# Block ends and two attention stages of a two-block transformer kernel: fewer column sums on TensorE, held-back first loads, queries loaded a stage early

## The chip, the cores and the metric

The kernel runs on one core of one Trainium2 chip as one program. The metric is the time of the whole program on the device in microseconds (us). The core has TensorE (matmuls, called PE in the profile, its weight loads PEld), VectorE (DVE), ScalarE (ACT), GpSimd (POOL) and SyncE (SP, which here only issues DMAs). Every engine runs its own list of instructions in order, and semaphores make them wait for each other.

## The reference, cut to what matters

Two blocks work on a sequence of 1024 tokens of width 1024 (`T` = 1024, `P` = 128). The first block runs twice (once with a recurrent mixer, once with a convolution mixer). Each of its two passes ends in the same few lines:

```python
h = layer_norm(DEEPNORM_ALPHA * h + mix @ w_out[i], ln_g[i], ln_b[i])
e = rms_norm(p[i] @ ple_w[i], ple_norm[i])
h = h + jax.nn.sigmoid(h @ ple_gate[i]) * e
```

`layer_norm` takes the mean and the mean square of the centred values over the 1024 channels; `rms_norm` takes the mean square of `p @ ple_w` over its 1024 channels.

The second block has two attentions side by side on the same input. `mla_attention` is causal attention with 8 heads of width 96. `nsa_attention` is the sparse one: 8 heads of width 64 in 2 groups, each query looks at compressed keys (made of windows of 32 tokens by a small two-layer network with weights `cmp_w1` and `cmp_w2`), at the 8 best blocks of 64 tokens, and at a window of 256 tokens; three gates mix the results:

```python
o = g[..., 0, :] * o_c + g[..., 1, :] * o_s + g[..., 2, :] * o_w
```

## The kernel before, in words

Everything is float32. Activations lie with channels on the 128 partitions and tokens along the free axis, so a sum over channels is a sum over partitions, which TensorE does with a matmul against a constant matrix `avg`. Large products use three matmuls of float32r parts (a high and a low part of weights and activations) for each tile; VectorE splits each weight tile (`divide`, lines 123 and 128). The program is a row of stages; between two stages stand a clearing of semaphores and a barrier of all engines.

**Block end** (`block_end`, line 5150; stage name `be`). It runs twice, near 1490 to 1755 us and near 2925 to 3195 us. TensorE does 24 products (`product`, matmuls on line 5250): 8 of `mix @ w_out` (g = 0 to 7, 48 matmuls each), 8 of `p @ ple_w` (g = 8 to 15, 12 matmuls each) and 8 of the gate (g = 16 to 23, 48 matmuls each). Around the middle the two norms are made:

- after product 8 a matmul with `avg` (line 5275) gives the mean, and VectorE subtracts it from the 8 tiles (line 5378);
- ScalarE squares each of the 8 centred tiles and each of the 8 tiles of `e` (`square`, line 5312), into one of two buffers `sq`. It also copies the 8 `e` tiles out of PSUM (`take_e`, line 5317);
- TensorE turns each of the 16 squared tiles into a column sum per 128 tokens: `add_squares` (line 5259) does 8 matmuls with the squares as weights and one column of `avg` as moving data. The layer norm's 8 go into `ln_cols`, the other 8 into `rm_cols`;
- when `ln_cols` is full, a small chain (VectorE line 5382, ScalarE square root line 5332, VectorE reciprocal line 5384) makes the factor, `spread` (line 5265, 8 matmuls) puts it on all partitions, VectorE multiplies the tiles (line 5395), ScalarE and VectorE make the high part (line 5322) and the low part (`lower_y`, line 5390) of each tile as moving data of the gate product.

The order on TensorE: product 8, mean, product 9, ten `add_squares` in a row (two of `e`, eight of the layer norm), product 10, `spread`, then products 11 to 15 with one `add_squares` after each, product 16 with the last one inside, second `spread`, products 17 to 23. A square may be written only after the buffer's last reader is done (`sq_used`).

**Dense attention** (`mla_select`, line 4135; stage name `mla`, 3806 to 4167 us). SP loads head 0's `q` and `k` (96 rows of 1024), the identity and the masks, head 0's `v`, then head 1, the weights of the compression (`w1` and others, 15 loads counted in `cmp_in`), heads 2 and 3, five tables and heads 4 to 7, without waiting. After that SP stores 16 output tiles as they come (`normed`). TensorE first makes the scores of units 0 and 1 (`row_scores`, lines 4368 and 4371); each waits for all three loads of its head, and its mask matmul for three small VectorE instructions (lines 4549 to 4551) that wait for identity and masks. Beside the attention, the compression (8 steps, line 4295) and the selection for the sparse attention run. POOL first issues two loads of queries for the selection, then sets the ones in `k` and `v`.

**Sparse attention** (`nsa_attention`, line 3799; stage name `nsa`, 4170 to 4580 us). SP loads `q` and `k` of both groups in 24 DMAs (lines 3887 and 3890, each row block twice, 6 MB in all). POOL loads identity, masks, `rows_in`, the selection, the gates, `v`, the compressed probabilities `pct` and `vc`. TensorE waits for the seven constants made by VectorE (`NMADE`) and for the first half of group 0's `q` and `k`, makes the first four chunks of scores (lines 3924 and 3929), and VectorE reduces each to maxima (lines 4020 and 4023) before the one PSUM buffer can be used again.

## Time and profile before

| | |
|---|---|
| median of 3 runs | 5513.8 us (5513.04 to 5519.81) |
| profiled execution | 5518.23 us, its span 5516.4 us |
| mean granted TensorE clock | 0.925 of full speed |
| PE busy | 88% of the span |
| DVE busy | 50% |
| ACT busy | 19% |

Times within the profile count from the span's start. The granted clock is 1.00 at 2.4 GHz and 0.50 at 1.2 GHz. A busy PE is not a PE at its peak: matmuls are pipelined, and one that waits for its weights counts as busy.

### The profile page before, as it was taken

To read this page: it belongs to the slowest core of one execution; us is meant where nothing else is said; L and a number is where in the kernel's file an instruction comes from. 1 tells how busy PE (TensorE), PEld (TensorE's weight loads), DVE (VectorE), ACT (ScalarE), POOL (GpSimd) and SP (SyncE) were. 2 spreads that over 40 slices of the span, in tenths; PEclk is the share of its full clock that TensorE was granted. 3 is DMA by queue.
4 is the path that set the end of the run, shared out by engine and by line. 5 is a ranking of instruction groups with operands and counts; after the bars stand their busy time and mean duration, and the time that the engine had idled before them with its cause. 6 is when DMAs were issued, how large, how long until landed. Compare 5 with 4: busy or idle time off the path is not lost. (4 is left out here: it accounts for less than half of the span.)

```text
span 5516.4 us, 89051 instructions
## 1 busy us (share of the span) xinstructions
PE 4851.6 (88%) x38472; PEld 3735.2 (68%) x38494; DVE 2746.4 (50%) x3664; ACT 1071.6 (19%) x1481; POOL 716.0 (13%) x646
## 2 busy tenths in 40 slices
PE   9996997999798997684867969998996998999999
PEld 7776887999586766343446847765653557788887
DVE  5776543444445886374664457232463335443332
ACT  2443221222321330000001221111221122110000
POOL 0002321111000460000000011011000000131330
PEclk9998998999789998796888889998997999999999
DMA  3443213111213333423223134136114004212213
GB/s 136 162 153 112 58 29 117 57 57 57 97 52 119 124 142 149 172 92 111 87 72 139 58 121 156 60 106 171 35 27 79 5 8 146 98 48 78 80 43 103
DMA packets 247271, 512.69 MB, mean 93 GB/s; under 512 B 35351, under 2 KB 118616, under 8 KB 246244
## 3 DMA queue, kind: packets, MB, share of 16 engines
q1 hardware_dynamic: 184580, 362.92, 20.3%
q0 software_dynamic: 31488, 110.53, 5.9%
q10 hardware_dynamic: 30816, 33.56, 1.7%
q8 instruction: 306, 5.01, 0.4%
q14 instruction: 81, 0.66, 0.0%
HBM read 353.70 MB, written 150.74 MB: 91 GB/s over the span
## 5 line engine op out<-in xcount | busy, mean ns | idle before, releaser
L4751 PE MATMUL tail_product<-tail_x_hi,tail_w_hi 128*128 128x512 f32 x832 | 329.0, 395 | 12.4 <-DVE tail_x_lo L128 10.8
L4751 PE MATMUL tail_product<-tail_x_lo,tail_w_hi 128*128 128x512 f32 x832 | 324.7, 390 | 0.0
L4751 PE MATMUL tail_product<-tail_x_hi,tail_w_lo 128*128 128x512 f32 x832 | 324.2, 390 | 0.0
L3501 PE MATMUL win_product<-kept_hn_hi,win_w_hi 128*128 128x512 f32 x560 | 229.1, 409 | 40.2 <-DVE win_w_lo L128 40.2
L1741 PE MATMUL front_product<-kept_x_hi,front_w_hi 128*128 128x512 f32 x544 | 221.1, 406 | 10.4 <-DVE kept_x_lo L128 10.1
L3501 PE MATMUL win_product<-kept_hn_hi,win_w_lo 128*128 128x512 f32 x560 | 220.3, 393 | 0.0
L3501 PE MATMUL win_product<-kept_hn_lo,win_w_hi 128*128 128x512 f32 x560 | 220.2, 393 | 0.0
L1741 PE MATMUL front_product<-kept_x_hi,front_w_lo 128*128 128x512 f32 x544 | 214.0, 393 | 0.0
L1741 PE MATMUL front_product<-kept_x_lo,front_w_hi 128*128 128x512 f32 x544 | 213.3, 392 | 0.0
L3155 PE MATMUL lc_ps<-idft,lc_zz 128*128 128x256 f32 x512 | 120.4, 400 | 91.2 <-DVE lc_zz L3033 91.2
L4751 PE MATMUL tail_product<-tail_f_hi,tail_w_hi 128*128 128x512 f32 x480 | 189.6, 395 | 0.0
L4751 PEld LDWEIGHTS tail_product<-tail_x_hi,tail_w_hi 128*128 128x128 f32 x832 | 156.7, 188 | 44.7 <-issue 11.5
L4751 PE MATMUL tail_product<-tail_f_hi,tail_w_lo 128*128 128x512 f32 x480 | 186.8, 389 | 0.0
L4751 PE MATMUL tail_product<-tail_f_lo,tail_w_hi 128*128 128x512 f32 x480 | 186.7, 389 | 0.0
L4751 PEld LDWEIGHTS tail_product<-tail_x_hi,tail_w_lo 128*128 128x128 f32 x832 | 156.5, 188 | 32.9
L2712 PE MATMUL oproj_product<-kept_h_hi,oproj_w_hi 128*128 128x512 f32 x384 | 156.0, 406 | 25.5 <-DVE kept_h_lo L128 20.6
L3155 PEld LDWEIGHTS lc_ps<-idft,lc_zz 128*128 128x128 f32 x512 | 103.3, 203 | 110.1 <-issue 94.4
L4751 PEld LDWEIGHTS tail_product<-tail_x_lo,tail_w_hi 128*128 128x128 f32 x832 | 156.7, 188 | 31.0 <-issue 0.2
L3501 PEld LDWEIGHTS win_product<-kept_hn_hi,win_w_hi 128*128 128x128 f32 x560 | 106.5, 190 | 89.4 <-DVE win_w_lo L128 41.1
L3142 PE MATMUL lc_ps<-lc_v,dft 128*128 128x512 f32 x256 | 123.1, 640 | 49.1 <-DVEq L2979 45.3
L3718 POOL DMA_DIRECT2D win_cq_hi_plain<-in_ada_w x16 | 11.7, 732 | 1152.9 <-POOLq L75 1081.3
L2093 POOL TENSOR_TENSOR rk_off<-rk_aa,rk_masks 128x1280 f32<-128x1280 f32 x32 | 99.1, 3113 | 422.7 <-DVE rk_aa L2257 422.7
(746 smaller groups left out, 11612.1 us busy)
## 6 DMA issues: line engine op xcount, KB each, us to landing
s_decayed<-front_ring SPq DMA_DIRECT2D x96, 256.0 KB, 3.9
tail_w<-in_w_gu SPq DMA_DIRECT2D x44, 512.0 KB, 3.2
win_w<-in_w_in SPq DMA_DIRECT2D x35, 512.0 KB
front_w<-in_even_w SPq DMA_DIRECT2D x34, 512.0 KB, 4.0
win_cq_hi_plain<-in_ada_w POOLq DMA_DIRECT2D x16, 1024.0 KB, 5.4
dn_kv<-s_qkv SPq DMA_DIRECT2D x16, 768.0 KB, 6.8
kept_held<-s_decayed SPq DMA_DIRECT2D x4, 3072.0 KB, 14.6
rk_in<-s_decayed SPq DMA_DIRECT2D x4, 3072.0 KB, 16.1
```

The lines of the kernel that those rows point to most:

```text
L1741: mm = pe.matmul(pp[:, u_, f, :], p, q, start=(k == 0 and m == 0), stop=(k == 7 and m == 2))
L2093: pool.tensor_tensor(off[d][:, 1:, :, :], turns[d][i % 2]["aa"][:, first, :].unsqueeze(1).to_broadcast([P, LV - 1, RPAIRS, RH]), masks[:, ...
L2712: mm = pe.matmul(pp[:, u, f, :], p, q, start=(k == 0 and m == 0), stop=(k == 7 and m == 2))
L3142: mm = pe.matmul(out[:, k, :], f(n), x[:, n, :], start=(j == 0), stop=(j == len(terms) - 1))
L3155: mm = pe.matmul(out[:, 2 * s + r // 2, r % 2 * 256:r % 2 * 256 + 256], zz[:, r, kind, f, ct * P:(ct + 1) * P], tabi[:, kind, f, r, :], st ...
L3501: mm = pe.matmul(pp[:, u, h, :], l, b, start=(k == 0 and m == 0), stop=(k == depth(s) - 1 and m == 2))
L3718: pool.dma_start(mw[:, n % 2, :, :, :], a["ada_w"][MOD_LO + MB * n:MOD_LO + MB * n + MB].rearrange("n p k m -> p n k m")).then_inc(mod_in[ ...
L4751: mm = pe.matmul(pp[:, s % 2, h_, :], l, b, start=(k == 0 and m == 0), stop=(k == deep(s) - 1 and m == 2))
```

## The change

**Block end.** ScalarE still squares the 8 centred tiles, the first into `acc`, the others into the two `side` buffers; VectorE adds them up in `acc` (7 additions, `add_y`). TensorE makes one column sum of `acc` (`sum_y`) in place of eight. The squares of `e` go to 8 tiles of their own (`e_sq`), which lie in the memory of the low parts `lo`; so `lower_y(k)` waits until `e_sq` tile k is summed. TensorE's new order: product 8, mean, products 9 to 15, `sum_y`, `sum_e` 0 and 1, `spread`, `sum_e` 2 to 4, product 16 with `sum_e` 5, 6 and 7 after its first three k steps, second `spread`, products 17 to 23. VectorE's splits of products 10 to 16 stand between subtractions and additions.

**Dense attention.** The first halves (512 tokens) of head 0's `q` and `k`, the identity and the masks are issued; SP then waits for the two halves, issues the second halves and `v` of head 0, waits for identity and masks, and goes on with head 1 and the rest. The scores of unit 0 wait only for the first halves. POOL sets all ones before it issues its two query loads. `w1` lies in a memory `room` shared with the next stage; before the store of unit 4, SP waits for the end of the compression (`h_mm`) and loads `q` and `k` of the sparse attention's group 0 into it (12 DMAs, 3 MB).

**Sparse attention.** Identity, masks and their bf16 copies are those of the stage before. Group 0's `q` and `k` are already there. POOL loads `rows_in`, selection and gates, waits for the last two, and then issues `v`, `pct` and `vc`. SP waits for `v` of group 0 and then loads group 1's `q` and `k`. TensorE waits for the (now five) constants only after the first four chunks of scores and the first turned maxima.

```diff
@@ Kept: the memory of lo gets a second name, lo_plain (plain float32) @@
@@ sparse attention @@
-        q = [st.sb(f"q{g}", [P, 4, T]) for g in range(2)]
-        k = [[st.sb(f"k{x}{g}", [P, T]) for x in range(2)] for g in range(2)]
+        q = [share.q, st.sb("q1", [P, 4, T])[:, :, :]]
+        k = [share.k, [st.sb(f"k{x}1", [P, T])[:, :] for x in range(2)]]
-                for x, y in ((ident[:, :], c["ident"]), (masks[:, :, :], c["att_masks"]), (rows_in[:, :, :], c["att_rows"])):
-                    pool.dma_start(x, y).then_inc(const_in, 16)
+                pool.dma_start(rows_in[:, :, :], c["att_rows"]).then_inc(const_in, 16)
                 pool.dma_start(sl[:, :, :, :], sel.rearrange("g p b n -> p g b n")).then_inc(lists_in, 16)
                 pool.dma_start(gt[:, :, :], gates.rearrange("(b p) n -> p b n", p=P)).then_inc(lists_in, 16)
+                pool.wait_ge(lists_in, 32)
...
+                sp.wait_ge(v_in[0], 32)
+                for h in range(2):
+                    share.load_queries(sp, q[1], k[1], qn, ksw, 1, h, qk_in[1][h])
...
-                pe.wait_ge(made, NMADE)
                 for x in early:
                     scores(x)
                 turn_maxima(0)
+                pe.wait_ge(made, NMADE)
...
-                dve.wait_ge(const_in, 48)
-                dve.tensor_copy(identb[:, :], ident[:, :]).then_inc(made, 1)
-                dve.tensor_copy(maskb[:, :, :], masks[:, 0:2, :]).then_inc(made, 1)
                 dve.tensor_copy(maskt[:, :, :, :], masks[:, 2:4, :].unsqueeze(2).to_broadcast([P, 2, 4, P])).then_inc(made, 1)
+                dve.wait_ge(const_in, 16)
                 dve.tensor_copy(rowb[:, :, :], rows_in[:, :, :]).then_inc(made, 1)
@@ new class AttentionShare @@
+        self.room = enter(nc.sbuf_tensor("att_room", [P, 2, 16, 256], F32))
...
+    def load_queries(self, sp, q, k, qn, ksw, g, h, sem):
+        cols = slice(h * H2, h * H2 + H2)
+        heads = qn.rearrange("(h d) t -> d h t", d=64)
+        for lo in (0, 64):
+            sp.dma_start(q[lo:lo + 64, :, cols], heads[:, 4 * g:4 * g + 4, cols]).then_inc(sem, 16)
+            for x in range(2):
+                src = ksw[x * P + 64 * g:x * P + 64 * g + 64, cols]
+                sp.dma_start(k[x][lo:lo + 64, cols], src).then_inc(sem, 16)
@@ dense attention @@
                 def head(h):
+                    lo = 0
                     if h == 0:
+                        sp.dma_start(q[0:96, 0, 0:H2], rows(qm, 0, 96)[:, 0:H2]).then_inc(first_in, 16)
+                        sp.dma_start(k[0:96, 0, 0:H2], rows(km, 0, 96)[:, 0:H2]).then_inc(first_in, 16)
                         sp.dma_start(ident[:, :], c["ident"]).then_inc(const_in, 16)
                         sp.dma_start(masks[:, :, :], c["att_masks"]).then_inc(const_in, 16)
+                        sp.wait_ge(first_in, 32)
+                        lo = H2
+                    sp.dma_start(q[0:96, h, lo:T], rows(qm, P * h, 96)[:, lo:T]).then_inc(head_in[h], 16)
+                    sp.dma_start(k[0:96, h, lo:T], rows(km, P * h, 96)[:, lo:T]).then_inc(head_in[h], 16)
...
                 head(0)
+                sp.wait_ge(const_in, 32)
                 head(1)
...
                 for u in range(NU):
+                    if u == 4:
+                        sp.wait_ge(h_mm, 1)
+                        for h in range(2):
+                            share.load_queries(sp, share.q, share.k, qn, ksw, 0, h, share.early_in[h])
                     sp.wait_ge(normed, u + 1)
...
-                queries(0)
-                queries(1)
                 for h in range(H):
...
+                queries(0)
+                queries(1)
...
-                    pe.wait_ge(head_in[h], 48)
+                    pe.wait_ge(first_in, 32)
+                    if u:
+                        pe.wait_ge(head_in[h], 48)
@@ block end, TensorE @@
+                def sum_y():
+                    pe.wait_ge(y_added, KT - 1)
                     for b in range(8):
+                        mm = pe.matmul(ln_cols[:, b:b + 1], acc[:, b * P:(b + 1) * P], avg[:, 0:1], start=(b == 0), stop=(b == 7))
+                    mm.then_inc(ln_summed, 1)
...
-                product(9)
+                for g in range(9, 16):
+                    product(g)
+                sum_y()
                 for j in range(2):
-                    add_squares(j, rm_cols, j == 0, False)
-                for k in range(KT):
-                    add_squares(2 + k, ln_cols, k == 0, k == KT - 1)
-                product(10)
+                    sum_e(j)
                 pe.wait_ge(ln_inv, 1)
                 pe.wait_ge(centred, KT)
                 spread(8, ln_spread)
-                for j in range(3, 8):
-                    product(8 + j)
-                    add_squares(7 + j, rm_cols, False, False)
-                product(16, (0, lambda: add_squares(15, rm_cols, False, True)))
+                for j in range(2, 5):
+                    sum_e(j)
+                product(16, lambda k: sum_e(5 + k) if k < 3 else None)
@@ block end, ScalarE @@
+                take_e(0)
+                for j in range(1, 5):
+                    square_y(2 * j - 2)
+                    take_e(j)
+                    square_y(2 * j - 1)
+                for j in range(5, 8):
+                    take_e(j)
@@ block end, VectorE @@
+                def add_y(k):
+                    dve.wait_ge(y_squared, k + 1)
+                    dve.wait_ge(y_added, k - 1)
+                    dve.tensor_tensor(acc[:, :], acc[:, :], side[:, k % 2, :], ALU.add).then_inc(y_added, 1)
                 for k in range(KT):
                     dve.tensor_tensor(res[:, k, :], res[:, k, :], flat(pm[:, :, :]), ALU.subtract).then_inc(centred, 1)
+                    if k % 2 == 1:
+                        divide(10 + k // 2)
+                    if k >= 3:
+                        add_y(k - 2)
+                for k in (6, 7):
+                    divide(8 + k)
+                    add_y(k)
+                divide(16)
...
                 def lower_y(k):
                     dve.wait_ge(upper_x, X0 + k + 1)
+                    dve.wait_ge(e_summed, k + 1)
```

## Rows read from the trace of the kernel before

**Rows 1.** The page: busy time and share of each engine, instructions.
```profile
PE 4851.6 (88%) x38472; PEld 3735.2 (68%) x38494; DVE 2746.4 (50%) x3664; ACT 1071.6 (19%) x1481; POOL 716.0 (13%) x646
```

**Rows 2.** Windows, block end: start:end length, busy PE PEld DVE ACT POOL, clock, DMA share, GB/s.
```profile
1587.00:1618.50 31.50, 31.06 (x161) 30.98 (x160) 7.83 (x10) 10.37 (x10) 0.00 (x0) 0.56 0.03 9
1624.90:1647.30 22.40, 22.40 (x140) 19.84 (x138) 17.98 (x22) 15.05 (x16) 0.00 (x0) 1.00 0.28 83
3028.50:3061.10 32.60, 32.16 (x162) 32.04 (x160) 7.86 (x10) 11.66 (x11) 0.00 (x0) 0.54 0.03 9
```

**Rows 3.** Groups by form, first block end: busy us, mean ns of one, idle before.
```profile
L5259 PE MATMUL be_ln_cols<-be_avg,kept_held 128*128 128x1 f32 x128 | 27.4, 352 | 0.0
...
L5395 DVE SCALAR_TENSOR_TENSOR kept_held<-kept_held,be_ln_g,be_pm 128x1024 f32<-128x1024 f32 x8 | 10.2, 1275 | 5.5 <-PE be_pm L5265 5.5
L5390 DVE SCALAR_TENSOR_TENSOR kept_mix_lo<-kept_held,be_ln_b,kept_mix_hi 128x1024 fp32r<-128x1024 f32 x8 | 10.1, 1279 | 0.0
```

**Rows 4.** Timeline, VectorE and ScalarE, first block end: start us, length us, engine, line.
```profile
1581.07 1.22 DVE L5374 TENSOR_TENSOR kept_held<-kept_held 128x1024 f32<-128x1024 f32 x1
...
1584.43 9.14 DVE L5378 TENSOR_TENSOR kept_held<-kept_held,be_pm 128x1024 f32<-128x1024 f32 x8 [1.47 <-PE be_pm L5275]
1593.49 0.29 DVE L123 CAST be_w_hi<-be_w 128x256 fp32r<-128x256 f32 x1
...
1594.15 0.28 DVE L123 CAST be_w_hi<-be_w 128x256 fp32r<-128x256 f32 x1
...
1660.64 1.02 ACT L5344 ACTIVATE kept_held<-be_ps 128x1024 f32<-128x1024 f32 x1 [3.99 <-PE be_ps L5250]
```

**Rows 5.** Timeline, TensorE, first block end: product matmuls at 1.2 GHz, spread, sum at 2.4 GHz.
```profile
1619.94 0.63 PE L5250 MATMUL be_ps<-be_p_hi,be_w_hi 128*128 128x512 f32 x1
1620.37 0.63 PE L5250 MATMUL be_ps<-be_p_lo,be_w_hi 128*128 128x512 f32 x1
...
1622.82 1.95 PE L5265 MATMUL be_pm<-be_ident,be_small 128*128 128x128 f32 x16
...
1627.40 1.84 PE L5259 MATMUL be_rm_cols<-be_avg,kept_held 128*128 128x1 f32 x16
```

**Rows 6.** Timeline, start of the dense attention: SP's issues, VectorE, TensorE's first mask.
```profile
3808.36 0.43 SPq L4220 DMA_DIRECT2D mla_masks<-in_c_att_masks  x1
...
3816.59 0.33 DVE L4549 CAST mla_identb<-mla_ident 128x128 bf16<-128x128 f32 x1 [34.54 <-DMA mla_masks<-in_c_att_masks]
...
3816.97 1.05 DVE L4551 TENSOR_SCALAR mla_negid<-mla_ident 128x128 f32<-128x128 f32 x1
...
3818.97 0.31 PE L4371 MATMUL mla_ps<-mla_maskb,mla_identb 128*128 128x128 bf16 x1
```

**Rows 7.** Tile view of the dense attention's query loads (256 KB each), last line.
```profile
DMA to landing us min/median/max: 3.5/3.7/8.6
```

**Rows 8.** Waits around the start of the sparse attention: total, times, longest.
```profile
PE nsa_ps L3924 <- DMA nsa_k<-s_ksw: 25.1, 1, 25.1
```

**Rows 9.** Timeline, start of the sparse attention: POOL's gates load, VectorE's first reduction.
```profile
4173.36 0.93 POOL L3872 DMA_DIRECT2D nsa_gates<-s_gates  x1
...
4189.89 0.42 DVE L4020 TENSOR_REDUCE nsa_bm<-nsa_ps 128x4 f32<-128x256 f32 x1 [8.77 <-PE nsa_ps L3929]
```

**Rows 10.** Tile view of the gates in the sparse attention, last line.
```profile
DMA to landing us min/median/max: 8.9/8.9/8.9
```

**Rows 11.** Windows: start of the sparse attention, and both attentions together.
```profile
4188.00:4222.00 34.00, 24.88 (x113) 11.46 (x114) 11.45 (x38) 3.22 (x4) 0.00 (x0) 0.60 1.03 192
3838.00:4580.00 742.00, 655.73 (x3380) 394.09 (x3402) 300.43 (x647) 154.47 (x246) 26.81 (x36) 0.90 0.17 36
```

**Rows 12.** Timeline, VectorE, dense attention: compression's end, output tiles of units 3 and 6.
```profile
3941.47 0.16 DVE L4539 COPY mla_pc<-mla_side 128x4 f32<-128x4 f32 x1 [3.17 <-PE mla_side L4295]
...
3952.68 0.68 DVE L4534 TENSOR_TENSOR mla_ob<-mla_po,mla_rs 64x512 f32<-64x512 f32 x1 [0.21 <-DVE mla_mx L4511]
...
3998.42 0.67 DVE L4534 TENSOR_TENSOR mla_ob<-mla_po,mla_rs 64x512 f32<-64x512 f32 x1
```

More of the change, by code:

```diff
@@ L89, in __init__ @@
         if split:
-            self.hi, self.lo = make("_hi"), make("_lo")
+            self.hi = make("_hi")
+            with nc.sbuf_tensor(f"kept_{name}_lo_plain", [P, tiles, T], F32) as plain:
+                self.lo_plain = plain
+            self.lo = make("_lo")
         else:
@@ L3796, in nsa_plan, with nsa_attention @@
     return units
-def nsa_attention(nc, tag, qn, ksw, vs, vw, sel, pct, vc, gates, c, dst):
+def nsa_attention(nc, tag, share, qn, ksw, vs, vw, sel, pct, vc, gates, c, dst):
     units = nsa_plan()
@@ L3856, in nsa_attention @@
         const_in, lists_in, cmp_in = st.sem("const_in"), st.sem("lists_in"), st.sem2("cmp_in")
-        qk_in = [st.sem2(f"qk_in{g}") for g in range(2)]
+        qk_in = [share.early_in, st.sem2("qk_in")]
         v_in = st.sem2("v_in")
@@ L4132, in mla_plan, with __init__, free, mla_select @@
     return units
-def mla_select(nc, tag, qm, km, vm, c, dst, qn, gates, k_src, v_src, a, table, vc_dst, pct_dst, sel_dst):
+class AttentionShare:
+    def __init__(self, nc):
+        self.ctx = ExitStack()
+        enter = self.ctx.enter_context
+        self.room = enter(nc.sbuf_tensor("att_room", [P, 2, 16, 256], F32))
+        self.ident, self.masks = enter(nc.sbuf_tensor("att_ident", [P, P], F32)), enter(nc.sbuf_tensor("att_masks", [P, 4, P], F32))
+        self.identb = enter(nc.sbuf_tensor("att_identb", [P, P], BF16))
+        self.maskb = enter(nc.sbuf_tensor("att_maskb", [P, 4, P], BF16))
+        self.early_in = [nc.alloc_semaphore(name=f"att_early_in{h}") for h in range(2)]
+        flat = self.room[:, :, :, :].rearrange("p m l c -> p (m l c)")
+        self.q = flat[:, 0:4 * T].rearrange("p (h t) -> p h t", t=T)
+        self.k = [flat[:, (4 + x) * T:(5 + x) * T] for x in range(2)]
+    def load_queries(self, sp, q, k, qn, ksw, g, h, sem):
[6 more added lines that the diff above has]
+                sp.dma_start(k[x][lo:lo + 64, cols], src).then_inc(sem, 16)
+    def free(self):
+        self.ctx.close()
+def mla_select(nc, tag, share, ksw, qm, km, vm, c, dst, qn, gates, k_src, v_src, a, table, vc_dst, pct_dst, sel_dst):
     H, NP, N2, NV = 8, 8 * QB, 2 * NCMP, 18
@@ L4168, in mla_select @@
         v = st.sb("v", [P, QB, H, P])
[L4169 to L4170 removed]
+        ident, masks, identb, maskb, negid = share.ident, share.masks, share.identb, share.maskb, st.sb("negid", [P, P])
         pt = st.sb("pt", [P, 3, H2])
@@ L4174, in mla_select @@
         kg = [st.sb(f"kg{m}", [P, 2, T]) for m in range(2)]
-        w1 = [st.sb(f"w1{m}", [P, 16, 256]) for m in range(2)]
+        w1 = [share.room[:, m, :, :] for m in range(2)]
         w2 = [st.sb(f"w2{m}", [P, 2, 64]) for m in range(2)]
@@ L5251, in product, with sum_e @@
                                                stop=(k == depth(g) - 1 and j == 2))
-                        if after and k == after[0]:
-                            after[1]()
+                        if after:
+                            after(k)
                     mm.then_inc(prod, 1)
-                def add_squares(q, out, first, last):
-                    pe.wait_ge(squared, q + 1)
+                def sum_y():
+                    pe.wait_ge(y_added, KT - 1)
                     for b in range(8):
-                        mm = pe.matmul(out[:, b:b + 1], sq[:, q % 2, b * P:(b + 1) * P], avg[:, 0:1], start=first and b == 0,
-                                       stop=last and b == 7)
-                    mm.then_inc(sq_used, 1)
+                        mm = pe.matmul(ln_cols[:, b:b + 1], acc[:, b * P:(b + 1) * P], avg[:, 0:1], start=(b == 0), stop=(b == 7))
+                    mm.then_inc(ln_summed, 1)
+                def sum_e(j):
+                    pe.wait_ge(e_squared, j + 1)
+                    for b in range(8):
+                        mm = pe.matmul(rm_cols[:, b:b + 1], e_sq[:, j, b * P:(b + 1) * P], avg[:, 0:1], start=(j == 0 and b == 0),
+                                       stop=(j == KT - 1 and b == 7))
+                    mm.then_inc(e_summed, 1)
                 def spread(col, done):
```

78 lines of the change are left out of this document (32 added, 46 removed).

## The prediction

> **What bounds the kernel now.** I read the page first: TensorE is busy for 88% of the span, no other engine for more than 50% [rows 1], so a change pays where TensorE stands still, runs at 1.2 GHz, or does cheap work at full price. Then the windows over the places that the diff touches, the groups there, the timelines for the order, and for the two attention starts the waits.
>
> *Block end.* From 1587.0 to 1618.5 TensorE is busy without a gap, at a granted clock of 0.56, and has nothing to show for it but ten column sums [rows 2]. Those of the layer norm take 27.4 us for eight, 3.42 us each [rows 3]; one at 2.4 GHz has 1.84 us to its last end [rows 5] and leaves TensorE after some 1.7. The sums bring about the low clock themselves: it was 1.00 when they began, and it came back only with product 10. The second block end repeats it (32.6 us at 0.54) [rows 2]. Later, products and single sums in turn keep the clock at 1.00 from 1624.9 to 1647.3 [rows 2]. VectorE does 7.8 us of work in the 31.5 us, so it has room for additions.
>
> *Dense attention.* The first mask matmul runs at 3818.97. VectorE's constants wait for the masks until 3816.59, a load issued at 3808.36: 8.2 us [rows 6]. The same load has ident, two whole heads' q and k, a head's v and 2 MB of weights around it. *Sparse attention.* TensorE idles 25.1 us for q and k [rows 8]; the first reduction on VectorE, which sets the pace of the early scores, starts at 4189.89 [rows 9], while the 16 DMA engines are full (share 1.03 at 192 GB/s) [rows 11].
>
> **Block end, step by step** (first one; the second is its copy). Before, VectorE starts subtracting at 1584.43 and product 16 ends at 1660.6, where ScalarE reads it [rows 4].
>
> New, up to `sum_y`: VectorE does 8 subtractions (9.14 us), 7 additions at 1.22 (8.5) and six splits at 0.66, from one start to the next (4.0) [rows 4]: 21.6 us, to 1606.0, plus about 2 of waiting for squares and products in this tight ring. The splits now stand between subtractions, so TensorE, which has 7 products of 12 matmuls (a product with its sum takes 22.4/5 = 4.5 [rows 2], less 1.7: 2.8 us), follows VectorE instead of leading. Split 15 waits for product 13, and products 14 and 15 end 5 us later: 1610.5.
>
> Then `sum_y` and two `e` sums. Before, the clock fell within about 4 us of such a run, so two are at 1.7 and one at 3: 1616.9. The eps, root and reciprocal chain hides behind the two `e` sums. The spread (1.7 us before its successor starts, 1.95 in all [rows 5]) doubles at 1.2 GHz: 1620.3. Before, it ended at 1624.5. So 4.2 us are won, and products 11 to 15 are done, but three `e` sums precede product 16 and three stand inside it. Two branches:
>
> - *Clock stays low.* 3 sums at 3.42: 1630.6. Three times 6 matmuls at 0.43 (from 1619.94 to 1620.37 [rows 5]) and a sum: 3 x (2.6 + 3.4) = 18.0, 1648.6. Then two k steps at 2.6 and three at 1.4 as the clock returns (before, a matmul every 0.43 us was still seen 2 us after product 10 began [rows 5]): 9.4, so 1658.0. Gain 2.6 us.
> - *Clock high from the spread on.* Spread to 1618.6. TensorE would need only 3 x 1.7 + 8 x 1.4 + 3 x 1.7 = 21.4, so VectorE is the bound: 8 turns and 8 low parts at 1.275 and 1.279 [rows 3], 1.2 from start to start, 19.2, a full-size split 1.9, the last k step 1.4: 1641.1. Gain 19.5 us. `lower_y`'s new wait for `e_summed` costs nothing here; in the low branch it holds the last two tiles for the sums, already in that sum.
>
> The trace of before shows neither run of sums next to a spread and a half-dense product, so both ends stand. A one in three weight on the high end (the spread is dense and may itself bring the clock back; product and sum in turn kept it high once it was) gives 0.33 x 19.5 + 0.67 x 2.6 = 8.2; I take 8.5. Two block ends: **17.0 us**. ScalarE's work is the same in another order, 16 squares and 8 copies; its root's table load hides. SP's weight loads go by the splits, which come no later than product 16 needs them.
>
> **Dense attention start.** The masks are again the fourth issue, at about 3808.36, now behind 0.4 MB and alone until the first halves have landed. A 256 KB load in the quiet part of this stage lands in 3.7 us, 8.6 at worst under load [rows 7]. So masks at 3812.1; identity, masks (now 512 columns, some 0.15 more) and negated identity take 1.43 [rows 6] plus 0.15: mask matmul at 3813.7 instead of 3818.97, **5.3 us**. Bounds: landing 3.5 and 8.6 give 5.5 and 0.4. Head 0's second halves and `v` are issued after 3811 and land by 3816 to 3817; TensorE reaches unit 1 at about 3818.3, four chunks later. Head 1 and the 15 compression loads start some 3 us later; they are needed when the compression starts, tens of us on, and were issued by 3829. POOL's two query loads wait behind 13 us of memsets and are first read at 3960: nothing. One more wait before each row score is already met, and TensorE's queue holds work.
>
> The Trainium skill, *DMA: Bandwidth & Descriptors*, section "Anatomy of one DMA — SWDGE (gpsimd) path", speaks against splitting head 0: each DMA pays about 2.0 us fixed beside bytes / 436e3. By that the masks would land 2.6 us after issue, an estimate that adds 1.1 us to the gain, and the halves' second fixed cost would fall after 3811, still before unit 1. This trace's own 3.7 us for 256 KB is above the page's 2.6, so the measurement is used.
>
> **Queries loaded early.** SP issues 12 DMAs (3 MB) after unit 3's store. The compression is over by 3941.5, where VectorE reads its sums, and unit 3's tile is ready at 3953.4 [rows 12]: no wait for it. At 192 GB/s [rows 11] 3 MB take 16 us, to about 3970. Behind them in SP's list stands the store of unit 4, whose buffer VectorE writes again for unit 6 at 3998.42 [rows 12]: 28 us of cover. Without it, each us would hold VectorE and then TensorE. The selection's loads and stores that share the engines then have a period of over 20 us to land. Nothing.
>
> **Sparse attention start.** q and k of group 0, identity and masks are there, so TensorE starts at once and stands at the one PSUM buffer until VectorE reduces. VectorE waits for `rows_in` and for selection and gates. Two loads vanish ahead of the gates, whose issue moves from 4173.36 [rows 9] to about 4172.3; landing at the quiet 3.7 us [rows 7]: 4176.0, first reduction 4176.1 instead of 4189.89: **13.8 us**. Bounds: the 8.9 us that the gates took before [rows 10] give 8.7; a landing in 1.9 us would leave VectorE's cast of `rows_in` as the bound, 15.2. What is late next: `v` of group 0, issued after 4176, is read 32 us after the first reduction, at 4208; even at 25 us it is there. `pct` and group 1 (5.5 MB together, 28 us at 192 GB/s) are in by 4211, before the first turn back at 4222. Group 1 is needed at half of the stage.
>
> **Sum.** 17.0 + 5.3 + 13.8 = 36.1 us from the profiled execution: 5518.2 - 36.1 = 5482.1 us. That execution lies 4.4 us above the median of 5513.8, so against the runs shown: **5477.7 us**.
>
> **Rivals.**
> - *Clock low in both block ends* (2.6 each): for it, ten sums in a row fell to 1.2 GHz in both, and six sums now follow each other within 20 us; against it, the dense spread between. 5513.8 - 5.2 - 19.1 = 5489.5.
> - *Clock high in both* (19.5 each): 5513.8 - 39.0 - 19.1 = 5455.7. For it, the steady 1.00 of mixed work; against it, three sums before the spread.
> - *The attention starts are bound by small loads anyway* (landings as under load: 0.4 and 8.7): 5513.8 - 17.0 - 9.1 = 5487.7. For it, the gates' tiny packets; against it, the emptied queues.
> - *Slower: the bodies of the attentions run at a lower clock.* Place: 742 us with a granted clock of 0.90 [rows 11], so 20% of them, 148 us, at 1.2 GHz; they hover near the level at which it falls, and everything in them shifts by 5 and 19 us with other traffic beside. Each us more at 1.2 GHz costs 0.5 where TensorE is the bound. From some 94 us more (a mean of about 0.845) the 36 us and 11 more are eaten; at 110 us more the time is 5477.7 + 55 = 5533. Against it: their instructions are the same.
>
> **How the numbers follow.** Forecast 0.46, low clock 0.25, high clock 0.14, starts bound by small loads 0.10, slower 0.05. The range 5456 to 5497 takes in the first four; below it lies half of the high case (0.07), above it the slower case and what the low clock and slow loads add up to together (0.05 + 0.05). 0.2% is 11 us, about what a measurement of this kernel can tell from no change: faster 0.93, same 0.02, slower 0.05.
>
> **What would show it.** Windows of each block end: between first subtraction and product 16's end 67.7 us instead of 76.2, a low clock from about the second `e` sum on, one `ln_cols` sum instead of eight, and products 9 to 15 paced by VectorE. First mask matmul of the dense attention 6.7 us after SP's issue of the masks gives 5.3; if it stays at 10.6, that step is wrong. Sparse attention: TensorE's 25 us wait ends at once, VectorE's first reduction some 5.6 us after SP's or POOL's first issue (19 before). The forecast is wrong if VectorE, waiting on squares, holds products 11 to 13 so long that the clock falls there too, or if a wait for `v` or `pct` appears after 4200.

## The result, and the profile after

The changed kernel takes 5478.4 us (median of 8 runs, 5466.3 to 5498.8) against 5513.4 us for the kernel before on the same chip (8 runs): ratio 0.9928, 95% interval 0.9914 to 0.9943. The forecast was 5477.7 us. On a second chip the ratio was 0.9944 (0.9924 to 0.9963).

The profiled execution took 5476.3 us, 42.0 less than that of before. The page shows TensorE as busy as before (88%, [rows 1]) over a shorter span:

```profile
span 5474.4 us, 88661 instructions
...
PE 4828.5 (88%) x38270; PEld 3702.4 (68%) x38270; DVE 2760.9 (50%) x3676; ACT 1070.3 (20%) x1481; POOL 713.9 (13%) x644
```

Stage by stage (first instruction to first instruction of the next), the first block end is 6.1 us shorter, the second 21.1, the dense attention 10.8, the sparse 13.2: 51.2 us. Stages whose code is untouched are 9.2 us longer (4.4 ahead of the first block end, 4.4 between the two, 0.4 elsewhere). In the twelve profiles of this study those same untouched stretches vary from 1479.1 to 1489.9 and from 1168.5 to 1175.9 us, so 9.2 is no more than chance gives, and part of the 51.2 may be chance too. One pair of profiles doesn't give the sum; the experiments do.

*Block ends.* Windows of the changed kernel (columns as in [rows 2]): from the first subtraction to the last product of the ring, then the sums with the spread, then up to the end of product 16; first block end, then the second.

```profile
1588.84:1614.90 26.06, 21.38 (x83) 16.21 (x82) 22.86 (x29) 20.01 (x21) 0.00 (x0) 0.93 0.20 62
1614.90:1625.20 10.30, 10.30 (x68) 10.25 (x67) 0.37 (x2) 2.12 (x3) 0.00 (x0) 0.72 0.17 52
1625.20:1660.60 35.40, 35.40 (x160) 32.29 (x161) 21.47 (x20) 11.71 (x11) 0.00 (x0) 0.65 0.05 15
3026.55:3050.90 24.35, 20.81 (x83) 15.71 (x82) 22.86 (x29) 20.02 (x21) 0.00 (x0) 0.93 0.21 66
3050.90:3060.20 9.30, 9.30 (x70) 9.22 (x68) 0.37 (x2) 3.52 (x4) 0.00 (x0) 0.82 0.15 56
3060.20:3086.80 26.60, 26.60 (x160) 24.32 (x160) 21.30 (x20) 11.71 (x11) 0.00 (x0) 0.87 0.06 20
```

The 31.5 us of sums at a clock of 0.56 [rows 2] are gone, and VectorE is busy for 22.86 us of the first window and paces it. The low clock itself isn't gone from the first block end. It has moved: TensorE spends as long a stretch without a gap at 1.2 GHz as before, now over the second sum of `e`, the spread, the other sums and the first three k steps of product 16 (a k step is six matmuls). The kernel before, then the changed one:

```profile
1590.95:1621.65 30.70, 30.70 (x139) 30.02 (x138) 4.25 (x9) 7.61 (x8) 0.00 (x0) 0.50 0.03 9
1619.34:1650.05 30.71, 30.71 (x128) 28.97 (x128) 19.91 (x17) 9.19 (x8) 0.00 (x0) 0.50 0.06 18
```

What differs between the two block ends is the third window: same work, 35.4 us at 0.65 against 26.6 us at 0.87. TensorE's timeline has the sums one by one (`ln_cols` is the layer norm's, `rm_cols` those of `e`, `pm` the spread):

```profile
1615.14 1.84 PE L5301 MATMUL be_ln_cols<-be_avg,kept_held 128*128 128x1 f32 x16
1616.84 4.70 PE L5307 MATMUL be_rm_cols<-be_avg,kept_mix_lo_plain 128*128 128x1 f32 x32
1621.41 3.76 PE L5313 MATMUL be_pm<-be_ident,be_small 128*128 128x128 f32 x16
1624.96 10.24 PE L5307 MATMUL be_rm_cols<-be_avg,kept_mix_lo_plain 128*128 128x1 f32 x48
...
3052.92 3.85 PE L5307 MATMUL be_rm_cols<-be_avg,be_lo_plain 128*128 128x1 f32 x32
3056.63 3.52 PE L5313 MATMUL be_pm<-be_ident,be_small 128*128 128x128 f32 x16
3059.99 7.34 PE L5307 MATMUL be_rm_cols<-be_avg,be_lo_plain 128*128 128x1 f32 x48
```

One layer norm sum at full clock (1.84 us) stands where eight took 27.4 [rows 3]. In both block ends the spread ran at 1.2 GHz (3.76 and 3.52, 1.95 before [rows 5]). Behind it the first stays there (48 matmuls in 10.24 us), the second returns part of the time (7.34). VectorE's rows give the lengths used below, first subtraction (`L5430`) to first scaled `e` (`L5468`), 71.8 and 60.3 us; in [rows 4]'s kernel they were 78.0 and 79.3.

```profile
1588.84 2.35 DVE L5430 TENSOR_TENSOR kept_held<-kept_held,be_pm 128x1024 f32<-128x1024 f32 x2 [1.48 <-PE be_pm L5323]
...
1610.62 1.22 DVE L5427 TENSOR_TENSOR kept_held<-kept_held 128x1024 f32<-128x1024 f32 x1
...
1651.83 1.28 DVE L5449 SCALAR_TENSOR_TENSOR kept_mix_lo<-kept_held,be_ln_b,kept_mix_hi 128x1024 fp32r<-128x1024 f32 x1 [3.29 <-PE be_rm_cols L5307]
...
1660.68 1.22 DVE L5468 TENSOR_TENSOR kept_held<-kept_held,be_pm 128x1024 f32<-128x1024 f32 x1 [7.01 <-PE be_pm L5313]
...
3026.55 2.35 DVE L5430 TENSOR_TENSOR be_res<-be_res,be_pm 128x1024 f32<-128x1024 f32 x2 [1.47 <-PE be_pm L5323]
...
3086.88 1.22 DVE L5468 TENSOR_TENSOR be_e<-be_e,be_pm 128x1024 f32<-128x1024 f32 x1 [5.02 <-PE be_pm L5313]
```

*Attention starts.* The timelines of the changed kernel answer to [rows 6] and [rows 9]. Dense: SP's first issue and that of the masks, VectorE's identity, TensorE's first mask. Sparse: POOL's first issue and VectorE's first reduction.

```profile
3788.59 0.33 SPq L4241 DMA_DIRECT2D mla_q<-s_qm  x1
...
3789.91 0.43 SPq L4244 DMA_DIRECT2D att_masks<-in_c_att_masks  x1
...
3792.97 0.40 DVE L4585 CAST att_identb<-att_ident 128x128 bf16<-128x128 f32 x1 [29.38 <-DMA att_masks<-in_c_att_masks]
...
3794.67 0.29 PE L4406 MATMUL mla_ps<-att_maskb,att_identb 128*128 128x128 bf16 x1 [2.14 <-DVE mla_negid L4587]
...
4141.73 0.53 POOL L3872 DMA_DIRECT2D nsa_rows_in<-in_c_att_rows  x1 [13.03 <-POOLq L75]
...
4146.04 0.42 DVE L4017 TENSOR_REDUCE nsa_bm<-nsa_ps 128x4 f32<-128x256 f32 x1 [0.95 <-DMA nsa_gates<-s_gates]
```

The row of the kernel before that belongs beside them is TensorE's first score matmul, ahead of the first mask matmul at 3818.97:

```profile
3818.38 0.80 PE L4368 MATMUL mla_ps<-mla_k,mla_q 96*128 96x128 f32 x2 [16.66 <-DMA mla_v<-s_vm]
```

There TensorE stood for head 0's `v` until 3818.38, while VectorE's last constant was ready at 3818.02 [rows 6]. With `v` landing when it did, sooner masks would have gained nothing without the other edit, by which unit 0's scores no longer wait for `v`.

The mask matmul comes 6.1 us after SP's first issue (11.9 before), the reduction 4.8 us after the stage's first instruction (19.4 before). Yet the first output tile of the dense attention is only 2.3 us earlier (47.0 after SP's first issue, 49.3 before), that of the sparse 11.2 (55.9, 67.1). The windows from each start to where the clock returns show why (PEclk is the column behind the five engines):

```profile
3788.60:3820.90 32.30, 26.25 (x59) 12.23 (x60) 8.69 (x17) 3.55 (x5) 13.36 (x18) 0.50 0.97 264
4141.24:4182.70 41.46, 29.77 (x122) 14.79 (x123) 16.91 (x44) 3.22 (x4) 8.55 (x11) 0.50 0.85 158
```

TensorE works at 1.2 GHz for 32.3 and 41.5 us from the start of the stage. Before, the clock returned 29.9 and 35.0 us after it. The first results come earlier by 5.8 and 14.6 us, the clock later by 2.4 and 6.5.

### The profile page after: what moved, and what is told of

Same layout as the page of the kernel before. It is cut to its first block and busy times, and to the rows that moved or that the text cites. A ratio compares the mean times of both kernels' runs of the same rounds, so it can differ in the third digit from the quotient of the medians.

```text
span 5474.4 us, 88661 instructions
## 1 busy us (share of the span) xinstructions
PE 4828.5 (88%) x38270; PEld 3702.4 (68%) x38270; DVE 2760.9 (50%) x3676; ACT 1070.3 (20%) x1481; POOL 713.9 (13%) x644
## 3 DMA queue, kind: packets, MB, share of 16 engines
q1 hardware_dynamic: 184804, 362.92, 20.5%
## 5 line engine op out<-in xcount | busy, mean ns | idle before, releaser
L1744 PE MATMUL front_product<-kept_x_hi,front_w_hi 128*128 128x512 f32 x544 | 220.4, 405 | 10.4 <-DVE kept_x_lo L131 10.2
L2715 PE MATMUL oproj_product<-kept_h_hi,oproj_w_hi 128*128 128x512 f32 x384 | 156.0, 406 | 24.7 <-DVE kept_h_lo L131 19.9
L2298 DVE TENSOR_TENSOR rk_x<-rk_x,rk_bankd 128x256 f32<-128x256 f32 x128 | 53.9, 421 | 203.4 <-PE rk_banka L2060 203.4
```

Source lines behind the costliest of these rows:

```text
L1744: mm = pe.matmul(pp[:, u_, f, :], p, q, start=(k == 0 and m == 0), stop=(k == 7 and m == 2))
L2298: dve.tensor_tensor(b["x"][:, :, :], b["x"][:, :, :], DD[:, first, :], ALU.add).then_inc(s["x_ready"], 1)
L2715: mm = pe.matmul(pp[:, u, f, :], p, q, start=(k == 0 and m == 0), stop=(k == 7 and m == 2))
```

## The experiments

For each run: median time of 4 to 8 executions and ratio to the kernel before on the same chip, and the lengths (us) read from its one profile. Block end: first subtraction to first scaled `e`. Dense: SP's first issue to the next stage's first instruction. Sparse: from there to the tail's.

| kernel | median us | ratio, 95% | block end 1 | block end 2 | dense | sparse |
|---|---|---|---|---|---|---|
| before | 5513.4 | 1 | 78.0 | 79.3 | 363.5 | 411.4 |
| changed | 5478.4 | 0.9928, 0.9914-0.9943 | 71.8 | 60.3 | 352.6 | 398.1 |
| block_only | 5495.7 | 0.9960, 0.9945-0.9975 | 71.8 | 63.5 | 366.8 | 406.4 |
| attention_only | 5494.7 | 0.9967, 0.9955-0.9979 | 78.0 | 79.3 | 351.8 | 392.6 |
| mixed_sums | 5461.3 | 0.9898, 0.9884-0.9913 | 63.2 | 63.8 | 352.7 | 392.6 |
| late_product15 | 5458.5 | 0.9886, 0.9871-0.9902 | 57.7 | 56.5 | 358.8 | 398.9 |
| changed_again | 5485.7 | 0.9944, 0.9924-0.9963 | 71.8 | 71.6 | 358.9 | 398.9 |
| no_holds | 5482.7 | 0.9947, 0.9930-0.9964 | 71.8 | 63.6 | 356.7 | 395.7 |
| queries_late | 5486.7 | 0.9946, 0.9927-0.9964 | 71.8 | 71.6 | 359.1 | 408.9 |
| kept_busy | 5447.2 | 0.9881, 0.9865-0.9897 | 57.4 | 57.6 | 355.5 | 393.1 |
| head2_earlier | 5455.5 | 0.9886, 0.9866-0.9905 | 57.1 | 57.4 | 352.2 | 393.6 |
| no_dense_fill | 5452.6 | 0.9876, 0.9856-0.9896 | 57.7 | 56.4 | 358.8 | 389.0 |

Each group of runs had its own runs of the kernel before, which took 5519.8 us beside block_only to late_product15, 5511.4 beside changed_again to kept_busy, 5517.3 beside the last two. Across groups the ratios are to be compared, not the times.

**block_only** (the kernel before with the hunks of the block end) and **attention_only** (with all others).

> The kernel before with the block-end part alone. In the profiled execution of the changed kernel the first block end ran from first subtraction to the first scaled e in 71.8 us (78.0 before) at a clock that stayed low from the first e sum on, the second in 60.3 us (79.3 before) with the clock high through most of it. Theory A: which of the two a block end gets is chance of the execution, so over many executions the part is worth about 2 x 12.6 = 25 us: median near 5488, and this profile shows again one length near 72 or one near 60, not something between. Theory B (as forecast): a low clock is the rule and 2.6 to 6 us each is what is normal, the second one's 19 being the exception; about 9 to 12 us, median near 5502, both lengths near 72 in this profile.

> The kernel before with the attention parts alone: first loads alone and the rest held back, group 0's queries loaded during the dense attention. In the changed kernel's profile the first mask matmul came 5.9 us earlier after SP's first issue than before, but the first output tile only 2.3 us earlier; the first reduction of the sparse attention came 14.6 us earlier, but its later tiles 11.2 us: the clock came back later by what was won. Theory A: the starts are worth 2.3 + 11.2 = 13.5 us and nothing else changes in the bodies on the mean: median near 5500. Theory B: the forecast, 5.3 + 13.8 = 19.1 us: 5494. Theory C: the bodies also gain (the dense attention's stage was 10.8 us shorter, the sparse one's 13.2): 24 us, 5489.

Measured: 24.1 and 25.1 us by medians, 22 and 18 us by the ratios, which add up to the changed kernel's 40 by its own. The lengths are again 71.8 and 63.5: for block_only theory B falls, since its 9 to 12 us lie outside the ratio's 14 to 30 us and the second block end isn't near 72. Theory A isn't whole either, as 63.5 lies between its two lengths. For attention_only the ratio's 12 to 25 us hold all three theories.

**changed_again** (no edit).

> The changed kernel, unaltered, for a second profile and its times beside the next three. Open is whether a block end's length is chance: so far the first was 71.8 us twice and the second 60.3 and 63.5. If chance decides, either can come out near 72 or near 61 here; if something in the first block end itself keeps the clock down, it is 71.8 a third time and the second again 60 to 64. Time 5480.

Measured: 71.8 in the first block end a third time (and in no_holds and queries_late), 71.6 in the second. So neither expectation holds whole: the first is the same each time, the second falls into two kinds. Beside it stands no_holds, whose block end has the same code. VectorE's first subtraction, first turned tile (a centred tile times the factor that the spread brings) and first scaled `e` in changed_again:

```profile
3024.24 2.35 DVE L5430 TENSOR_TENSOR be_res<-be_res,be_pm 128x1024 f32<-128x1024 f32 x2 [1.47 <-PE be_pm L5323]
...
3061.00 3.66 DVE L5454 SCALAR_TENSOR_TENSOR be_res<-be_res,be_ln_g,be_pm 128x1024 f32<-128x1024 f32 x3 [6.49 <-PE be_pm L5313]
...
3095.84 1.22 DVE L5468 TENSOR_TENSOR be_e<-be_e,be_pm 128x1024 f32<-128x1024 f32 x1 [8.15 <-PE be_pm L5313]
```

and in no_holds:

```profile
3026.09 2.35 DVE L5426 TENSOR_TENSOR be_res<-be_res,be_pm 128x1024 f32<-128x1024 f32 x2 [1.47 <-PE be_pm L5319]
...
3062.91 3.66 DVE L5450 SCALAR_TENSOR_TENSOR be_res<-be_res,be_ln_g,be_pm 128x1024 f32<-128x1024 f32 x3 [6.54 <-PE be_pm L5309]
...
3089.66 1.22 DVE L5464 TENSOR_TENSOR be_e<-be_e,be_pm 128x1024 f32<-128x1024 f32 x1 [5.14 <-PE be_pm L5309]
```

Up to the first turned tile they are the same to 0.06 us (36.76 and 36.82); behind it they take 34.84 and 26.75. In the second the clock came back for the sums inside product 16, in the first it didn't. What decides between two executions that are equal so far, no run shows.

**mixed_sums.** The six `e` sums stand singly behind products instead of around the spread.

```diff
                 for g in range(9, 16):
                     product(g)
+                    if g >= 10:
+                        sum_e(g - 10)
                 sum_y()
-                for j in range(2):
-                    sum_e(j)
+                sum_e(6)
...
-                for j in range(2, 5):
-                    sum_e(j)
-                product(16, lambda k: sum_e(5 + k) if k < 3 else None)
+                product(16, lambda k: sum_e(7) if k == 0 else None)
```

> The changed kernel with the same products and sums in another order: six e sums stand one by one behind products 10 to 15, one behind the layer norm's sum, the last in product 16, so that no run of e sums stands around the spread. Theory A (sums in a row are what brings the low clock, the block end then pays it until product 16): the clock is high from the spread on in both block ends, both lengths near 59 to 61 us, some 10 us less in all than the changed kernel: 5468. Rival: TensorE then has 29.8 us of work before the layer norm's sum (7 products at 2.8, 6 sums at 1.7) where VectorE needs 23, so the spread comes 6 us later and nothing is won: 5478 or some us above, however the clock stands.

Measured: both block ends 63 to 64 us, not 59 to 61; ratio 0.9898, below the changed kernel's interval. Theory A's mechanism didn't show: with single sums the clock was low too, for 17.1 us in the first block end and 20.5 in the second, from the sum behind the layer norm's into product 16 (with a break of 3.4 us in the first). The first one's spread, and the first matmul of product 16 behind it:

```profile
1617.37 3.53 PE L5313 MATMUL be_pm<-be_ident,be_small 128*128 128x128 f32 x16
...
1626.01 0.77 PE L5292 MATMUL be_ps<-kept_mix_hi,be_w_hi 128*128 128x512 f32 x1 [5.11 <-DVE kept_mix_lo L5448]
```

The rival has its part: the first turned tile comes 37.8 and 38.9 us after the first subtraction (36.4 and 33.7 in the changed kernel). Behind it 25.4 and 24.9 us are left, where the changed kernel takes 35.4 and 26.6, though TensorE stood 5.1 us for VectorE's tiles at a low clock. By these profiles what costs the changed kernel is how many sums still stand behind the spread when the clock is low (six, up to 3.4 us each; one here), not the low clock alone. Whether sums in a row bring it about stays open.

**late_product15.** Four sums behind products 10 to 13, one behind the layer norm's sum, product 15 behind the spread.

```diff
-                for g in range(9, 16):
+                for g in range(9, 15):
                     product(g)
+                    if 10 <= g < 14:
+                        sum_e(g - 10)
                 sum_y()
-                for j in range(2):
-                    sum_e(j)
+                sum_e(4)
...
-                for j in range(2, 5):
-                    sum_e(j)
-                product(16, lambda k: sum_e(5 + k) if k < 3 else None)
+                product(15)
+                sum_e(5)
+                product(16, lambda k: sum_e(6 + k) if k < 2 else None)
@@ ScalarE: take_e(7) stands ahead of upper_y(2) @@
```

> The changed kernel with four e sums behind products 10 to 13, one behind the layer norm's sum, and product 15 moved behind the spread (its e tile is taken between the centred tiles' copies), then one sum and the last two in product 16. TensorE has 6 products and 4 sums, 23.6 us, before the layer norm's sum, no more than VectorE's 23, and dense work right behind the spread while VectorE turns the first tiles. Theory A: clock high from the spread on and the spread no later than in the changed kernel: lengths near 55 to 57 us, 5460. Rival: ScalarE's extra 2 us between the copies, or product 15 ahead of product 16, delays product 16: lengths near 60, 5470 as with mixed sums.

Measured: 57.7 and 56.5, the first turned tile at 32.7 and 31.6, and 56.4 to 57.7 in the six block ends of its three descendants. The spread still ran at 1.2 GHz, in 3.76 us; the clock was low for 6.8 us around it in the first block end and for 3.4 in the second, and product 15 behind it began at 1.2 GHz at 1626.70 and ran at 2.4 GHz from 1627.97 on.

```profile
1623.29 3.76 PE L5313 MATMUL be_pm<-be_ident,be_small 128*128 128x128 f32 x16
...
1626.70 0.77 PE L5292 MATMUL be_ps<-be_p_hi,be_w_hi 128*128 128x512 f32 x1
...
1627.97 0.40 PE L5292 MATMUL be_ps<-be_p_hi,be_w_hi 128*128 128x512 f32 x1
```

The windows of the first block end, ring with most of the spread, then the rest:

```profile
1594.49:1622.00 27.51, 27.17 (x162) 23.72 (x161) 23.14 (x31) 20.25 (x22) 0.00 (x0) 0.98 0.21 60
1622.00:1652.00 30.00, 27.51 (x148) 23.53 (x149) 21.30 (x20) 13.41 (x13) 0.00 (x0) 0.90 0.10 34
```

So theory A's lengths came out, but not its clock from the spread on.

This kernel beats the changed one on both chips: 0.9886 against 0.9928 and 0.9944, 23 to 32 us below the changed one. The code of its attentions is the changed kernel's.

**no_holds.** Four waits out: `sp.wait_ge(first_in, 32)` and `sp.wait_ge(const_in, 32)` (dense), `pool.wait_ge(lists_in, 32)` and `sp.wait_ge(v_in[0], 32)` (sparse).

> The changed kernel with the order of its loads kept but every hold taken out: SP doesn't wait for the first halves nor for identity and masks, POOL doesn't wait for selection and gates, SP not for v of group 0. Theory A (the holds are what makes the first loads quick): the masks land near 7 us after their issue instead of 3, first mask matmul near 10 us after SP's first issue (6.1 with the holds, 11.9 before), and the first reduction of the sparse attention near 10 us after the stage's first issue (4.8 with, 19.4 before), since the gates took 8.9 us before beside full queues. Rival (the order and the early queries are enough): both within 1 us of the changed kernel. The time differs by 5 us or so either way.

Measured: first mask matmul 6.7 us after SP's first issue (6.1 with the holds), masks landing in 3.5 us instead of 3.0: in the dense attention order and halves do it, not the hold. In the sparse one the gates take 8.4 us to land instead of 3.0, and the first reduction comes 10.2 us after the stage's first instruction instead of 4.8:

```profile
4157.77 0.42 DVE L4015 TENSOR_REDUCE nsa_bm<-nsa_ps 128x4 f32<-128x256 f32 x1 [2.49 <-DMA nsa_gates<-s_gates]
```

But the first output tile is only 0.5 us later (56.5 against 56.0): 5.4 us of head start are worth half a microsecond. In this profile the clock returned 24.7 us after the start (and fell once more for 6.8 us), not after 41.5, which is the likely reason. The reduction's delay didn't reach the first output tile.

**queries_late.** The 12 loads of group 0 are issued by SP at the start of the sparse attention again, ahead of the hold.

> The changed kernel with group 0's q and k loaded at the start of the sparse attention again (SP's first 12 DMAs, 3 MB), the holds kept. Theory A: TensorE waits for the first half of group 0 (1.5 MB, 8 us at 192 GB/s and some issue time) and the gates land beside it: first reduction 10 to 13 us after the stage's first issue, the first output tile near 62 to 64 (56.0 with early queries, 67.1 before), so early loading is worth 6 to 8 of the 11 to 15 us. Rival: POOL's held loads alone do it, first reduction under 7. The dense attention's length stays near 352 either way, as the early loads cost nothing there.

Measured: first reduction at 14.7 us and first output tile at 66.0, both later than theory A had them, the stage 408.9 us, which is what it took before (411.4, 406.4). TensorE's wait for the queries is back:

```profile
PE nsa_ps L3923 <- DMA att_room<-s_ksw: 20.3, 1, 20.3
```

So the early queries carry the gain of the sparse attention nearly whole (10 of the 11.2 us at the first output tile, all of it at the stage's end), and they cost the dense one nothing: 359.1 us without them, 358.9 with. That is read from one profile each; the times (0.9946 here, 0.9944 for changed_again) don't show the 10 us, which is as much as their intervals leave open.

**kept_busy.** late_product15 with matmuls whose result is never read, at both starts.

```diff
@@ dense, TensorE; hot is zeroed by VectorE @@
+                    for _ in range(n):
+                        pe.matmul(pt_ps[:, 0, :], hot[:, 0:P], hot[:, P:5 * P], start=True, stop=True)
...
+                keep_busy(14)
                 for x in ITEMS[0:item_no[("turn", 0, 0)]]:
                     row_scores(x)
+                    keep_busy(1)
@@ sparse, TensorE @@
-                for x in early:
+                for n, x in enumerate(early):
                     scores(x)
+                    for _ in range(4 if n else 16):
+                        pe.matmul(pst[:, 0, :], identb[:, :], maskb..., start=True, stop=True)
```

> The kernel late_product15 with additional matmuls whose result is never read, at both attention starts: in the dense one 14 of 512 bf16 columns while TensorE waits for the first loads and one behind each of the first chunks of scores; in the sparse one 16 behind the first chunk of scores and 4 behind each other early one. Theory A (the starts are long because TensorE stands still, so its clock is 1.2 GHz when the loads are there, and the thin early work doesn't bring it back for another 26 and 36 us): the clock is back within some 8 us, the first output tile of the dense attention comes near 36 us (46.8 now), that of the sparse near 46 (56.1 now), and the time falls by 15 to 20 us below late_product15, though there are more matmuls. Rival: the clock isn't what limits the starts, or falls again at once; then the added matmuls cost 2 to 6 us each.

Measured: the first output tiles come at 37.0 (46.8 in late_product15) and 49.4 (56.1). The windows over the first 36.0 us of the dense attention, late_product15 and then kept_busy, have 0.55 and 0.93 for the clock:

```profile
3773.38:3809.40 36.02, 29.97 (x75) 14.51 (x76) 9.63 (x19) 4.21 (x7) 13.36 (x18) 0.55 0.98 268
```

```profile
3759.60:3795.62 36.02, 34.65 (x135) 17.64 (x136) 15.25 (x26) 6.72 (x12) 13.36 (x18) 0.93 0.98 261
```

The clock and the first tiles are as theory A has them. The gain of 15 to 20 us is not there: the fourth dense output tile is at 141.5 instead of 142.2, the two stages are 3.3 and 5.8 us shorter in the profile, and the ratio 0.9881 isn't told apart from 0.9886. TensorE caught up with the loads (head 2 lay behind 5 MB), and fell back to 1.2 GHz:

```profile
PE mla_ps L4405 <- DMA mla_v<-s_vm: 2.3, 1, 2.3
```

**head2_earlier** (kept_busy with `head(2)` between `weights(0)` and `weights(1)`) and **no_dense_fill** (that without the added matmuls of the dense attention).

> kept_busy with one more move: head 2 of the dense attention is loaded between the two weight sets of the compression instead of behind both. In kept_busy the first output tile came 9.8 us earlier than in late_product15, but the second only 4.3: TensorE stood 2.3 us for head 2, whose loads lay behind 5 MB, and ran at 1.2 GHz for 6.8 us after it. Theory A (the start had caught up with the loads): no wait, no low clock there, second tile at 55.5 after SP's first issue instead of 61.0, fourth near 136 instead of 141.5, the compression as early as before since its loads have 20 us to spare; 4 to 6 us less, 5442. Rival: the loads fill the 16 DMA engines to 75 us after the first issue in any order, and what head 2 wins, head 3 or the compression pays; fourth tile at 141, 5447.

> head2_earlier without the additional matmuls in the dense attention; those in the sparse one stay. Theory A (low clock limits the dense start, the added matmuls are worth about 10 us there once head 2 is in time): first output tile back at 46.8, fourth at 142, 6 to 10 us slower than head2_earlier: 5450. Rival (the dense attention is paced by something later, as in kept_busy, where it was only 3.3 us shorter): within 3 us of head2_earlier.

Measured: by the first tiles in the profiles theory A holds for both: second and fourth dense tile at 55.4 and 135.7 with head 2 earlier, 65.3 and 142.1 without the added matmuls. By the end of the stage 6.6 us of that are left (352.2, 358.8), and the times, 0.9886 and 0.9876, don't show even those (theory A had no_dense_fill 6 to 10 us slower). Whether the added matmuls are worth anything stays open: these times can't tell 0.2%.

## Why the prediction was right

The time was right to 0.7 us. So close a hit is luck: the terms were off by up to 5 us each. Means over the profiles with unaltered code of a part (five for each), before over its two:

| term | forecast | measured |
|---|---|---|
| two block ends | 17.0 | 6.2 + 13.2 = 19.4 |
| dense attention | 5.3 | 365.2 - 355.0 = 10.2 |
| sparse attention | 13.8 | 408.9 - 396.2 = 12.7 |
| sum | 36.1 | 42.3 |

By the times the sum is 35 (medians), 40 (ratio) and 31 (ratio on the second chip); 42.3 lies in the first ratio's interval (31 to 47) and just outside the second's (20 to 42).

- *Block end up to the spread:* right step by step in its times. VectorE's ring ended 23.0 us after the first subtraction (forecast 23.6), the layer norm's sum began at 26.3 (26.1), the spread at 32.6 (32.5) and ended at 36.1 (35.9). One thing that the forecast names as a sign of being wrong did happen, in small: TensorE stood 2.2 us for VectorE's split before product 12 and again before product 13, and the clock was low for 3.4 us in the latter. The layer norm's sum came only 0.2 us later than forecast.

```profile
1605.22 0.50 PE L5292 MATMUL be_ps<-be_p_hi,be_w_hi 128*128 128x512 f32 x1 [2.17 <-DVE be_w_lo L131]
...
1606.31 0.63 PE L5292 MATMUL be_ps<-be_p_hi,be_w_hi 128*128 128x512 f32 x1
```

- *The branches:* the low one was priced too dear. It gave 6.2 us instead of 2.6, since the clock came back as the last sum inside product 16 began (it took 2.01 us, not 3.4), not two k steps behind it. The wait of the last low parts for the sums is there (3.29 us, row 1651.83). In the second block end 71.6 stands for low, 60.3 and 63.5 for mostly high; fully high, as forecast (58.5 in this measure), was never seen in the changed order. The weights, one in three for high, came near in the sum of both, though nothing in the forecast sets the two block ends apart: 0 of 5 in the first block end, 3 of 5 in the second. The rival "low in both" was the state of two of five profiles, "high in both" of none.
- *Dense start:* the first mask matmul came 5.8 us earlier as forecast (5.3), but only in part for the reason given (masks in 3.0 us instead of 8.2): before, TensorE's own wait for `v` ended later still (row 3818.38), and the forecast passed over it. The 5.3 are measured against 3818.97, 0.95 us after VectorE's last constant; from that constant its own terms give 4.3. The 6.7 us that it names as a sign count from SP's first issue, the 10.6 beside them from the masks' issue. The hold I credited is worth 0.6 us. That the 5.3 reach the end of the stage was the step that failed: 3.5 were paid back within the first 33 us by a clock that returned later (attention_only kept 5.7), and some 7 came from the stage's body, where the 1.2 GHz stretches were fewer. Which edit does that no run isolates; open.
- The Trainium skill's *DMA: Bandwidth & Descriptors*, section "Anatomy of one DMA — SWDGE (gpsimd) path", gives 2.6 us for the masks by its fit, which is an estimate. They took 3.0 with 0.4 MB beside them, nearer to the page than to the 3.7 of the row of before, and 3.5 without the hold, nearer to the row.
- *Queries early:* right, no cost in the dense attention.
- *Sparse start:* size right (14.6 at the first reduction, 12.7 over the stage), reason half right. I had the gates' landing as what ends last. For the first reduction that is so; for the first output tile it isn't, as no_holds shows (0.5 us): what counts is that the queries are there (10 us in queries_late).
- *Slower rival:* it didn't happen. The granted clock over the dense stage was 0.89 before and 0.90 to 0.91 after, over the sparse one 0.88 and 0.89 to 0.91. No wait for `v` or `pct` appeared.

## What to carry to other kernels

A wait that is taken away at a place where TensorE's clock is low is worth what the clock then does, not the wait: follow the gain to the stage's next output before counting it. Put thin TensorE work (column sums) singly between dense products and ahead of the step on which everything waits, keep a dense product for behind that step, and move additions to an engine with room. When two profiles are compared, subtract the untouched stages first; here they moved by 9 us beside a difference of 42.

## What the runs showed of the hardware

- TensorE that is busy almost without a gap stayed at 1.2 GHz for long: 26 us of score matmuls in the dense start, 31 us of sums, spread and product 16 in the first block end. In kept_busy fourteen dense matmuls whose result nobody reads ahead of the first scores had 2.4 GHz back 4.7 us after SP's first issue, against 32.1 us in late_product15.
- Two executions that agree to 0.06 us over 36.8 us took 34.8 and 26.8 us for the same instructions behind it. A single profile of such a stretch says little; the second block end, with the same code, was 60.3, 63.5, 63.6, 71.6 and 71.6 us.
- The load of the gates took 3.0 us with the loads behind it held back and 8.4 us beside them (no_holds). The first reduction came 5.4 us later for it, the stage's first output tile 0.5.
